# A kernel of three model blocks on one Trainium2 core: filling products in quarters during attention 2, another order of inputs and of the output tail

## What is computed

```python
def odd_mixer(y, cos, sin, w_in, b_in, sinks, w_out, b_out):   # "attention 2"
    proj = y @ w_in + b_in
    q, k, v, z = jnp.split(proj, ...)
    attn = sliding_window_gqa_sinks(rotary(q), rotary(k), v, sinks)
    return (attn * jax.nn.silu(z)) @ w_out + b_out
...
h = h + (p[i] @ w_ple_proj[i]) * sigmoid(rmsnorm(h) @ w_ple_gate[i])
return rmsnorm(h, final_norm_w)                                 # the output tail
```

## Time and profile before

| | |
|---|---|
| median of three runs | 3276.26 us (3274.48 to 3281.40) |
| the profiled execution, its own time | 3271.06 us |
| its span | 3269.3 us |
| mean granted TensorE clock | 0.982 |
| TensorE busy | 3121.4 us, 95% |
| VectorE, ACT, POOL busy | 1631.0, 1148.6, 959.1 us |
| the stretch of attention 2, from first scores on | about 1878.5 to 2095.0 us |

### The profile page before, as it was taken

How to read it: one execution, slowest core, us unless ns; L and a number is a source line. 1 busy time by engine, 2 the same in 40 slices (tenths; PEclk the granted TensorE clock), 3 DMA queues, 4 the chain that set the end, 5 groups by cost and what they waited for, 6 DMA issues and landing times.

```text
span 3269.3 us, 38359 instructions
## 1 busy us (share of the span) xinstructions
PE 3121.4 (95%) x15508; PEld 2456.0 (75%) x15508; DVE 1631.0 (50%) x2683; ACT 1148.6 (35%) x1948; POOL 959.1 (29%) x699
## 2 busy tenths in 40 slices
PE   8999989999989999999999978899999999899998
PEld 6776667666878888777887755678778888788876
DVE  6969651112446654242332367667555545533435
ACT  2115553112441121113341176446446422322334
POOL 4211001112416785125421112321111223442522
PEclk9999989999999999999999989999999999999999
DMA  4110001112422232114321101331011144433322
GB/s 125 52 32 20 14 14 45 39 52 84 142 73 82 83 110 83 50 45 142 123 88 39 39 26 52 113 96 39 27 46 46 54 117 120 129 135 110 103 72 102
DMA packets 251057, 242.25 MB, mean 74 GB/s; under 512 B 15360, under 2 KB 198016, under 8 KB 249856
## 3 DMA queue, kind: packets, MB, share of 16 engines
q1 hardware_dynamic: 228944, 195.52, 19.9%
q10 hardware_dynamic: 21936, 44.27, 3.9%
HBM read 201.03 MB, written 38.73 MB: 73 GB/s over the span
## 4 chain that ended last, share of the span: by engine, by line
PE 82%; DVE 6%; ACT 5%; DMA 2%; POOL 2%; issue 1%; SPq 1%; ACTq 0%; DVEq 0%
PE psum L541 22%; PE psum L543 21%; PE psum L542 21%; PE psum L659 3%; PE psum L547 3%; DMA arena<-in_w_in 2%; PE psum L705 1%; PE psum L731 1%; DVE arena L2806 1%; PE psum L1172 1%; PE psum L842 1%; PE psum L1123 1%; POOL WS L3100 1%; DVE arena L2696 1%; PE psum L1122 1%
## 5 line engine op out<-in xcount | busy, mean ns | idle before, releaser
L3100 POOL TENSOR_TENSOR WS<-arena,WS 128x1024 fp32r<-128x1024 f32 x271 | 676.9, 2504 | 1854.6 <-ACT WS L1188 1854.6
L541 PE MATMUL psum<-XH,WS 128*128 128x512 f32 x2464 | 987.4, 401 | 36.0 <-POOL XL L3156 15.7
L543 PE MATMUL psum<-XH,WS 128*128 128x512 f32 x2464 | 963.9, 391 | 0.0
L542 PE MATMUL psum<-XL,WS 128*128 128x512 f32 x2464 | 963.9, 391 | 0.0
L541 PEld LDWEIGHTS psum<-XH,WS 128*128 128x128 f32 x2464 | 465.2, 189 | 151.1 <-issue 30.3
L543 PEld LDWEIGHTS psum<-XH,WS 128*128 128x128 f32 x2464 | 465.0, 189 | 99.4
L542 PEld LDWEIGHTS psum<-XL,WS 128*128 128x128 f32 x2464 | 465.5, 189 | 96.8 <-issue 4.8
L1188 ACT ACTIVATE WS<-arena 128x1024 fp32r<-128x1024 f32 x271 | 284.4, 1058 | 688.2 <-PE psum L543 248.6
L541 PE MATMUL psum<-WS,XH 128*128 128x512 f32 (+1 forms) x1024 | 397.0, 388 | 19.3 <-DVE XL L2131 7.2
L542 PE MATMUL psum<-WS,XH 128*128 128x512 f32 (+1 forms) x1024 | 393.8, 385 | 0.0
L543 PE MATMUL psum<-WS,XL 128*128 128x512 f32 (+1 forms) x1024 | 393.6, 384 | 0.0
(11 more groups left out here) (296 smaller groups left out, 3234.5 us busy)
## 6 DMA issues: line engine op xcount, KB each, us to landing
arena<-in_w_in SPq DMA_DIRECT2D x85, 512.0 KB, 3.9
arena<-in_w_out SPq DMA_DIRECT2D x48, 512.0 KB, 3.4
arena<-in_w_in_even SPq DMA_DIRECT2D x48, 512.0 KB, 4.2
arena<-in_w_out_even SPq DMA_DIRECT2D x32, 512.0 KB, 3.3
h_spill<-arena ACTq DMA_DIRECT2D x24, 512.0 KB, 3.2
arena<-s_table SPq DMA_DIRECT2D x8, 1536.0 KB, 6.8
arena<-in_w_in_odd SPq DMA_DIRECT2D x18, 512.0 KB, 3.9
s_table<-arena SPq DMA_DIRECT2D x32, 256.0 KB, 2.9
```

The source lines that it names most:

```text
L541: e.matmul(ps, wh, xh, start=start, stop=False)
L542: e.matmul(ps, wh, xl, start=False, stop=False)
L543: return e.matmul(ps, wl, xh, start=False, stop=stop)
L3100: e.tensor_tensor(lo, raw(book.raw_of.get(("w", u), 0), kbs, n), hi.bitcast(F32), SUB).then_inc(*w.up("w_lo", u))
```

## The change

It has three parts. **Start:** ACT issues x of half 0 (even kb) and cols before anything else; SP issues one weight block, x of half 0 (odd kb), the second weight block, x of half 1 whole, and then the other constants, which now belong to "b1_cst". TensorE no longer waits for "fix"; it runs the first two weight blocks (glu_b and glu_a of m = 0) together through proj_first, both over half 0 and then both over half 1. proj_first takes the number of blocks from its list in every program. VectorE subtracts all of x, POOL none. **Attention 2:** a filling tile is cut in four pieces of six products (fine = True yields after every second kb, or after each of the four weight blocks of an output tile), and PIECES says how many come in each tick: one in ticks 1 to 16, two in 17 to 24, one in 25 to 32, two in 33 to 36. The other engines step piece by piece before the next tick. Weight loads come one at a time, in the ticks of LOADS, and SP starts two blocks early after every fourth (ahead). Frees of the last tile come one per piece. **Tail:** the root is parted from the square (fin_root), and the next tile's sigmoid stands between them; VectorE takes h4 of the next tile before the mean of this one; the last tile is scaled and stored in two halves.

The diff, cut to its core (the same steps of POOL's and VectorE's fill, and proj_first's lengths in the other programs, are left out):

```diff
@@ -161,6 +161,12 @@
         return u
+    def ahead(self, n):
+        for _ in range(n):
+            self.start(self.next)
+            self.next += 1
@@ -356,7 +362,8 @@
 XS3 = view(84, 4, S)
-FILL = (1, 3, 5, 7, 17, 19, 21, 23, 27, 30, 33, 34)
+PIECES = [0] + [1] * 16 + [2] * 8 + [1] * 8 + [2] * 4
@@ -366,12 +373,19 @@
     return ([1], 128) if UNITS[u][0] == 0 else ([0, 1], 0)
-def attention2(tick, fill, late):
+LOADS = (6, 10, 14, 17, 25, 26, 27, 28)
+def attention2(tick, fill, late, loads=iter(())):
     for u in range(37):
+        for _ in range(PIECES[u - 1] if late and u else 0):
+            next(fill)
         tick(u)
-        if u - late in FILL:
-            next(fill, None)
+        for _ in range(LOADS.count(u)):
+            next(loads, None)
+        for _ in range(0 if late else PIECES[u]):
+            next(fill)
@@ -590,6 +604,8 @@
                     ws.free()
+                if fine and k + per < 8:
+                    yield
@@ -678,8 +694,9 @@
     ws.pump(2)
-    w.wait_ge("fix")
-    for m in range(4):
+    proj_first([((f"glu_{ab}", 0, 0), w_in[:, c:c + 128], lambda half, done=done: [(done, 0, half)])
+                for ab, c, done in (("b", 2560, "glu_sig"), ("a", 2048, "glu"))], "b1", None, None)
+    for m in range(1, 4):
@@ -879,16 +896,18 @@
     late = [load_w(w2[:, 1792 + 128 * i:1920 + 128 * i], 8, 128) for i in range(4)]
-    def z_tile(i, half, ring):
+    def z_tile(i, half, ring, fine=False):
...
+            if fine and kb % 2 and kb < 7:
+                yield
         t.then_inc(*w.up("z2o_ps", 4 + i, half, also=[("w_used", u)] if half else []))
     for i in range(4):
-        z_tile(i, 0, pb)
+        run(z_tile(i, 0, pb))
@@ -940,13 +959,13 @@
         for i in range(4):
-            z_tile(i, 1, b7)
+            yield from z_tile(i, 1, b7, fine=True)
...
-                ready=lambda tile: ("odo", tile)) for ch in range(2)]), 0)
+                ready=lambda tile: ("odo", tile), fine=True) for ch in range(2)]), 0)
@@ -1320,29 +1342,24 @@
                              scale=gcol(kb)).then_inc(*w.up("x_hi", stage, kb, hf))
-    e.dma_start(cols, ap["cols"]).then_inc(*w.landed("fix", 0))
-    e.dma_start(ident, cst_in("ident")).then_inc(*w.landed("fix", 1))
-    e.dma_start(ones, cst_in("ones")).then_inc(*w.landed("fix"))
-    e.dma_start(m01, cst_in("m01")).then_inc(*w.landed("b1_cst", 0))
-    e.dma_start(mneg, cst_in("mneg")).then_inc(*w.landed("b1_cst", 1))
-    e.dma_start(vb1, row_in("v1")).then_inc(*w.landed("b1_cst"))
-    ws.pump(2)
+    for kb in range(0, 8, 2):
+        e.dma_start(XSTAGE[:, kb, half_of(0)], ap["xT"][tile_of(kb), half_of(0)]).then_inc(*w.landed(f"x_in{kb}_0"))
+    e.dma_start(cols, ap["cols"]).then_inc(*w.landed("fix"))
     for half in range(2):
-        for kb in range(0, 8, 2):
-            e.dma_start(XSTAGE[:, kb, half_of(half)], ap["xT"][tile_of(kb), half_of(half)]).then_inc(
-                *w.landed(f"x_in{kb}_{half}"))
-    for half in range(2):
+        ws.pump(half + 1)
...
-    for m in range(4):
-        def sig(_, half):
-            w.wait_ge("glu_b", m, 0, half)
-            e.activation(C5[:, m + 1, 30 + 512 * half:542 + 512 * half], ps_of("glu_b", m, 0, half), ACT.Sigmoid,
-                         bias=col("b_in", 20 + m)).then_inc(*w.up("glu_sig", m, half))
-        run(proj_cm(1, sig))
+    def glu_sig(m, half):
+        w.wait_ge("glu_b", m, 0, half)
+        e.activation(C5[:, m + 1, 30 + 512 * half:542 + 512 * half], ps_of("glu_b", m, 0, half), ACT.Sigmoid,
+                     bias=col("b_in", 20 + m)).then_inc(*w.up("glu_sig", m, half))
+    run(proj_first([lambda half: glu_sig(0, half), lambda half: None], None, None))
+    for m in range(1, 4):
+        run(proj_cm(1, lambda _, half: glu_sig(m, half)))
@@ -1716,22 +1733,23 @@
         for i in range(4):
+            for _ in range(3):
+                yield
             z_ev(4 + i, 1)
             ws.free()
-            if i == 3:
-                for _ in range(4):
-                    ws.load()
...
-                if tile == 3:
-                    for _ in range(4):
+                for _ in range(4):
+                    if tile == 3:
                         ws.free()
-                    if ch == 0:
-                        for _ in range(4):
-                            ws.load()
-                yield
-    attention2(tick, fill(), 1)
+                    yield
+    def loads():
+        for _ in range(8):
+            ws.load()
+            yield
+    attention2(tick, fill(), 1, loads())
@@ -2077,7 +2095,11 @@
             w.wait_ge("nrm_rc", "fin", tile - 2)
-        rms("fin", tile, H3[:, tile, :], SQ3[tile % 2], small[:, 32 + tile:33 + tile])
+        e.activation(SQ3[tile % 2], H3[:, tile, :], ACT.Square, accum_out=small[:, 32 + tile:33 + tile]).then_inc(
+            *w.up("nrm_sq", "fin", tile))
+    def fin_root(tile):
+        rms_root("fin", tile, small[:, 32 + tile:33 + tile])
@@ -2088,10 +2110,15 @@
         fin(tile)
+        fin_root(tile)
     weave((proj_tm(512, tiles=range(4, 8)), 1, True), (g_evs(8, 4), 1, True))
-    for k in range(4):
-        g_ev(12 + k)
+    g_ev(12)
+    for k in range(3):
         fin(4 + k)
+        g_ev(13 + k)
+        fin_root(4 + k)
+    fin(7)
+    fin_root(7)
@@ -2198,7 +2225,7 @@
     for half in range(2):
-        for kb in range(1, 8, 2):
+        for kb in range(8):
@@ -3074,21 +3103,27 @@
         e.tensor_tensor(o, o, sg, A_).then_inc(*w.up("h4", ch, tile))
-    def fin(tile):
-        r, hx = small[:, 32 + tile:33 + tile], H3[:, tile, :]
+    def fin(tile, parts=1):
+        r, step = small[:, 32 + tile:33 + tile], 1024 // parts
...
-        e.scalar_tensor_tensor(hx, hx, r, G3, M, M).then_inc(*w.up("fin", tile))
+        for i in range(parts):
+            sl = slice(step * i, step * i + step)
+            hx = H3[:, tile, sl]
+            e.scalar_tensor_tensor(hx, hx, r, G3[:, sl], M, M).then_inc(
+                *w.up("fin", tile, i, also=[("fin", tile)] if i == parts - 1 else []))
...
-    for k in range(4):
-        h4(12 + k)
+    h4(12)
+    for k in range(3):
+        h4(13 + k)
         fin(4 + k)
+    fin(7, 2)
@@ -3149,13 +3184,8 @@
     ws.pump(2)
-    for half in range(2):
-        for kb in range(0, 8, 2):
-            w.wait_ge("x_hi", "b1", kb, half)
-            sl = half_of(half)
-            e.tensor_tensor(XL[:, kb, sl], XSTAGE[:, kb, sl], XH[:, kb, sl].bitcast(F32), SUB).then_inc(
-                *w.up("x_lo_p", "b1", kb, half, also=[("x", "b1", kb, half)]))
-    run(proj_cm(12))
+    proj_first(2)
+    run(proj_cm(10))
@@ -3375,12 +3406,17 @@
         load_raw(src, kbs, n, key, ("raw_used", n_raw[0]))
-    ws.pump(2)
     for half in range(2):
-        for kb in range(1, 8, 2):
-            e.dma_start(XSTAGE[:, kb, half_of(half)], ap["xT"][tile_of(kb), half_of(half)]).then_inc(
-                *w.landed(f"x_in{kb}_{half}"))
-    run(proj_cm(12))
+        ws.pump(half + 1)
+        for kb in range(8):
+            if half or kb % 2:
+                e.dma_start(XSTAGE[:, kb, half_of(half)], ap["xT"][tile_of(kb), half_of(half)]).then_inc(
+                    *w.landed(f"x_in{kb}_{half}"))
+    for i, (dst, name) in enumerate(((ident, "ident"), (ones, "ones"), (m01, "m01"), (mneg, "mneg"))):
+        e.dma_start(dst, cst_in(name)).then_inc(*w.landed("b1_cst", i))
+    e.dma_start(vb1, row_in("v1")).then_inc(*w.landed("b1_cst"))
+    proj_first(2)
+    run(proj_cm(10))
@@ -3452,21 +3488,24 @@
         for i in range(4):
+            for _ in range(3):
+                yield
             ws.free()
-            if i == 3:
-                for _ in range(4):
-                    ws.load()
...
-                if tile == 3:
-                    for _ in range(4):
+                for _ in range(4):
+                    if tile == 3:
                         ws.free()
-                    if ch == 0:
-                        for _ in range(4):
-                            ws.load()
-                yield
-    attention2(lambda u: None, fill(), 1)
+                    yield
+    def loads():
+        for k in range(8):
+            ws.load()
+            if k % 4 == 3:
+                ws.ahead(2)
+            yield
+    attention2(lambda u: None, fill(), 1, loads())
@@ -3544,10 +3583,13 @@
     run(proj_tm(512, tiles=range(4, 8)))
-    for tile in range(8):
+    for tile in range(7):
         w.wait_ge("fin", tile)
         e.dma_start(out[tile_of(tile), :], H3[:, tile, :]).then_inc(*w.landed("out", tile))
-    w.wait_ge("out", 7)
+    for half in range(2):
+        w.wait_ge("fin", 7, half)
+        e.dma_start(out[tile_of(7), half_of(half)], H3[:, 7, half_of(half)]).then_inc(*w.landed("out", 7, half))
+    w.wait_ge("out", 7, 1)
```

(26 more changed lines are left out.)

## The result

The changed kernel takes **3231.01 us** (median of four runs, 3225.74 to 3234.76) against 3275.37 before on the same chip: the ratio is 0.9866, with a 95% interval of 0.9854 to 0.9877. The forecast was 3234, the range 3222 to 3249. The profiled execution took 3234.76 us with a span of 3232.9.

What follows compares the result with a forecast made beforehand. TensorE, busy 95% of the span, was taken as the bound, its idle or half-speed time as the prize. Gains of 5.7 (start), 31 (attention 2) and 5.5 (end) sum to 42 off the 3276.3 median: 3234 us, range 3222 to 3249.

Steps and rivals of the forecast that it cites:

- Rival B: Start stays bound by DMA: first product at 14 or half 1 late, gain 1 there, 3239 us; chance 0.07.
- Work: Attention 2: TensorE's full-clock products, from full ticks, four short ticks and 12 filling tiles, 161.9 us together.
- Waits: Attention 2: TensorE's idle time apart from the last tile's wait, 15.6 us instead of 39.2.
- The first divide: Attention 2: TensorE waits for VectorE's first divide in a short tick with one quarter, 1.9 us.
- Bank 7: Attention 2: waits for ACT's Silu to free the bank after each z tile, 1.75 then three of 0.7, 3.9 us.
- The tile turn: Attention 2, tick 35: one tile turn without a tick between, VectorE's add and signals, 1.2 us.
- POOL's subtractions: Attention 2: POOL's subtractions hold up VectorE and so TensorE, 8.6 us, bounds 3 and 24.
- The last tile: End of attention 2: wait behind two weight blocks on ACT and POOL, 4.7 us (4.0 to 5.3) instead of 5.29.
- Half clock and rounding: Attention 2: time lost to half clock, with rounding, 3.2 us instead of 10.1, bounds 1 and 10.
- A: Attention 2's one-quarter ticks: ACT and POOL become the bound, idle 27 or more, 3246 us; chance 0.17.
- D: Attention 2's closed gaps open again behind it, VectorE's normalization chain setting the time: gain 11 to 20, 3260 us; chance 0.04.
- C: Attention 2: clock falls amid the cut-up work; 3315 us if half of it runs at half clock; chance 0.02.

Runs made afterwards that it cites:

- e4: The changed kernel run once more, unchanged; 3231.48 us, ratio to the kernel before 0.9871.
- e7: The changed kernel with two quarters in every second tick instead of one in each, in attention 2's one-quarter stretches; 3239.26 us, ratio 0.9901.
- e9: The changed kernel with ACT's and POOL's last attention tick before the weight blocks, and eight attention-block subtractions moved from POOL to VectorE; 3218.13 us.
- e3: The kernel before with the new tail alone; 3266.84 us, ratio 0.9977.
- e6: The changed kernel with quarters kept but weight loads back in lumps, four at tick 17 and four at tick 24; 3233.46 us, ratio 0.9878.
- e2: The kernel before with the new start alone (order of inputs and proj_first); 3266.22 us, ratio 0.9974.

## Why the prediction was right, and where it was off

**The sum.** 42 was forecast and 44.4 measured by the medians. The three parts are independent, as the sum took them, and each lies where it was put: 5.7 forecast and 7.5 measured alone, 31 and 30.3, 5.5 and 6.9, where a single part is known to some 3 us. That the total is met within 3 us is in part luck: by the profiles the gain was 36.4 (39.7 with e4's), because the start (4.6 for 5.7), attention 2 (28.4 for 31) and half clock outside of them (-2.3 for 0) each took 1 to 3 us of what was promised; the medians hide this, as the profiled execution of before lies under its median and that of after over it. The range was also narrower than its working: the bounds given for the parts of attention 2, all taken at their bad end together, leave a gain of 3 us there, not 18.

**Start.** The forecast had the first rounding at 5.43, or at 6.0 if w0 shares the queues, and its 10.0 takes the 6.0. The question was right and the answer early: the rounding comes at 5.86 to 7.13. Everything behind it was priced well, 4.18 from the rounding to the first product where 4.0 stood (1.06, 0.53 and VectorE's 2.43 under POOL's lock). No wait follows until 60, so half 1 was there in time. Rival B's case, a first product at 14 or half 1 late, did not come; the start is still bound by a transfer, that of w0, and its landing varies by 1.3 us.

**Attention 2.** 185.4 was forecast; it took 188.1, in e4 186.7. By its terms in after:
- Work was 161.9; it is 167.4. This is the term that was mis-sized most. A piece alone costs 1.59 (1905.18 to 1906.77), two together 2.94 (6.05 - 3.11), where a quarter tile was put at 1.42. With 24 single and 12 double groups that is 24 x 1.59 + 12 x 2.94 = 73.4 instead of 12 x 5.66 = 67.9. e4 confirms it: 167.75 us busy at a clock of 1.00. Two groups of one piece take 3.18 where one group of two takes 2.94, so each further group of 512-column products between the small ones costs TensorE about 0.24 us; there were 12 groups and are 36, and 24 x 0.24 is the 5.5 within rounding. Most of it lies at the group's two ends: products follow one another at 0.23 inside it, and at 0.33 behind the first (1905.18 to 1905.51) and behind the last (1906.44 to 1906.77). The 0.17 in e7's expectation is 1.59 - 1.42, which is not yet the price of a group, since the 1.42 has its share of a tile's own two ends.
- Waits were 15.6 by the sum; they are 13.5 (18.8 idle less the 5.30). The first divide was 1.9 and measured 2.23. Bank 7 was 3.9 and measured 2.8, its first wait 1.27 and not 1.75. The tile turn was 1.2 and measured 0.78. POOL's subtractions, 8.6 in the sum, make up the rest, about 7.4, in the places where they were looked for: 1.70 and 1.69, then 1.08, 1.11 and 1.11 from 2009.91 on.
- The last tile was 4.7 and measured 5.30, the upper bound.
- Half clock and rounding were 3.2; 169.3 - 167.4 leaves 1.9, in e4 0.3: the difference is the half clock behind the first divide's 2.23.

The errors (+5.5, -2.1, +0.6, -1.3) add up to the 2.7. One reading of the kernel before was off: at 1942 ACT waited for no transfer. It rounded two blocks (from 1935.68), and the 6.75 are VectorE's 2.20 and a divide of 5.23 under POOL's three subtractions; late transfers belong to the 10.22 alone.

The page SBUF — State Buffer of the Trainium skill (SBUF: two separate sides) has VectorE and GpSimd exclude each other on a shared port pair. The long operations of after and e9's POOL row of 3.54 agree. What did not follow is the 24 us that each blocked operation would cost TensorE: a stall of VectorE costs TensorE only what exceeds the slack of its tick, a wait of 1.70 for 3.1 us of stall, and of 0.32 where the same two subtractions fall into a tick with two pieces (1961.75).

**Tail.** 5.5 forecast, 5.7 by the profile, 6.9 by e3's median. One statement was wrong: that 23 us pass behind the last product of the kernel before. The earlier trace rows themselves have TensorE busy for 9.07 us of these 23. It did no harm to the sum, since ACT's chain was the bound then. It would have told that the new rounds of 5.1 meet TensorE's tile of 5.4: the last round is 5.43, its sigmoid waits 0.75 for TensorE, and a shorter chain on ACT could win nothing more in that round.

**The rivals.** A (ACT and POOL as the bound, idle 27 or more) did not come: 13.5. D (the gaps open again behind the stage) did not: after is ahead of before by 2.2 us at the stage's start, by 30.1 at 2143.27 and by 31.8 at 2825.47. C (the clock falls in the quartered work) did not either: 0.99 over the stage, transposes at 1.07 behind a wait of 1.70; the one fall, behind the first divide, is gone after 5 us. The Trainium skill's rule of micro-idles between groups (TensorE: Matmul & The Clock Gate, A second HAM failure mode) did not decide here; whole tiles with their empty ticks had 0.93.

**Of what was to show it,** the first product (11.11 for 10.0), no wait until 60, the stage (188.1 for 185) and its largest inner wait (2.23, below 3) came as said. Ticks take 4.69 and not 4.5, the last round 5.43 and not 5.1, VectorE's last scaling ends at 3229.8 and not near 3224 (3226.4 in e4), and the transposes are not at 1.06 throughout: those behind the 2.23 stand at the start of 5 us of half clock.

**What stays open.** Why e6's lumps cost only some 3 us: neither the frees of the last tile nor the early starts of SP were taken back in a run. Why the half clock behind one wait of 2.2 to 2.4 us comes and behind another does not.

## What to carry to other kernels

Cut filler work so that every step of a latency-bound loop gets some of it: the smallest amount that makes the filled engine the slower one (here 1.59 us on 3.10, against VectorE's 3.77) closes most of the waits, and pays about 0.24 us for each extra group. Look also at the order of the final step: work put ahead of it on ACT and POOL is a wait for TensorE, and taking away 4.8 us of it here gave 7.4, the clock's part included. A stall of a neighbour costs what it exceeds the slack by, so put POOL's subtractions into the steps with the most slack, and not several into one (three in one tick: 5.29 in e6, 6.75 before).

## What the runs showed of the hardware

- **The total moves with the granted clock.** Executions of e2 took 3255.48 us at a mean clock of 0.984 and 3269.65 at 0.979; time times clock is 3203 and 3201. Where the times of one kernel differ much, the product differs less: over 11 runs of e2 by 6.0 us where the times differ by 14.8, over 9 runs of e3 by 2.6 where they differ by 10.9. Where they differ by less than 5 it tells nothing (e4: 6.7 and 4.8; e6: 8.3 and 4.7), as the clock is given in steps worth 3.2 us. A part worth 3 us is better seen in the profile's own stretch than in the total.
- **Not every wait costs the clock.** Transposes took 1.06 to 1.12 behind waits of up to 2.40 in some ticks of e7 and 1.94 behind one of 2.42 in another; a wait of 2.23 at the same place was followed by half clock in after and not in e4. 5.3 us was followed by half clock in each profile that had it.
- **Excluding works both ways**: VectorE's four divides 3.14 instead of 1.14, POOL's subtraction 3.54 instead of 2.36. The same subtraction of 128x1024 takes VectorE 1.22.
